# Expert outputs weighted at their PSUM copy and added to a sum in DRAM by accumulating indirect DMAs

## The reference, cut to what matters

```python
combine = route(h, w_router, router_bias)   # 512 x 16: two experts per token, weights sum to 1
ffn = 0
for e in range(16):                         # D_EXPERT = 256
    a = silu(h @ w_gate[e]) * (h @ w_up[e])
    ffn = ffn + combine[:, e:e + 1] * (a @ w_down[e])
ple = sigmoid(h @ w_ple_gate) * (p @ w_ple_proj)
x = layer_norm(alpha * h + ffn + ple, g, b)
```

## Time and profile before

| | us |
|---|---|
| runs (three) | 538.92, 539.41, 539.88 |
| span of the profiled execution, the only time known of it | 537.8 |
| PE busy | 479.0 (89%) |
| DVE busy | 312.9 (58%) |
| ACT busy | 170.4 (32%) |
| POOL busy | 145.7 (27%) |
| DMA | 98.95 MB, mean 184 GB/s |

### The profile page before, as it was taken

The page is one execution under the profiler, slowest core; times in us unless marked ns, Lnnn a source line. Parts: engine busy times, 40 slices in busy tenths (PEclk is TensorE's granted clock), DMA queues, the critical chain, the costliest instruction groups (busy, mean ns, idle before and its releaser), DMA issues.

```text
span 537.8 us, 4916 instructions
## 1 busy us (share of the span) xinstructions
PE 479.0 (89%) x1742; PEld 271.6 (50%) x1742; DVE 312.9 (58%) x516; ACT 170.4 (32%) x259; POOL 145.7 (27%) x138
## 2 busy tenths in 40 slices
PE   6999959999998999999999999899999999998100
PEld 2444436456853454444345444666766766675000
DVE  0289995934596226675072223477667757756197
ACT  0310002033569500003000003655555465452061
POOL 5018300360197550002000640023223223201032
PEclk9999979999999989999998999999999999999755
DMA  8991014212788591012700036699999999600353
GB/s 281 377 287 25 0 39 55 48 24 90 285 293 334 202 402 41 39 40 68 283 1 1 0 71 257 214 340 357 332 357 370 334 346 375 247 18 14 137 220 157
DMA packets 37303, 98.95 MB, mean 184 GB/s; under 512 B 16960, under 2 KB 22672, under 8 KB 30864
## 3 DMA queue, kind: packets, MB, share of 16 engines
q1 hardware_dynamic: 28272, 88.50, 45.3%
q0 software_dynamic: 5088, 8.49, 4.6%
q10 hardware_dynamic: 3920, 1.66, 1.4%
HBM read 91.18 MB, written 14.17 MB: 196 GB/s over the span
## 4 chain that ended last, share of the span: by engine, by line
PE 69%; DVE 19%; DMA 5%; ACT 3%; issue 3%; SPq 1%; DVEq 0%; POOLq 0%; ACTq 0%
PE bank L992 11%; PE bank L921 10%; PE bank L1069 8%; PE bank L1049 8%; PE bank L798 4%; PE bank L1055 3%; PE bank L1034 3%; PE bank L781 3%; PE bank L1057 3%; DMA region_b<-in_ssm_par 3%; PE bank L995 3%; PE bank L845 2%; PE bank L1052 2%; DVE region_f L1556 2%; PE bank L915 1%
## 5 line engine op out<-in xcount | busy, mean ns | idle before, releaser
L992 PE MATMUL bank<-region_c,region_g 128*128 128x512 f32 x128 | 58.2, 609 | 0.0
L921 PE MATMUL bank<-region_b,region_e 128*128 128x512 f32 x128 | 57.7, 609 | 0.0
L781 PE MATMUL bank<-region_e,region_a 128*128 128x512 f32 x128 | 55.4, 593 | 0.0
L992 PEld LDWEIGHTS bank<-region_c,region_g 128*128 128x128 f32 x128 | 24.6, 195 | 30.7 <-issue 30.7
L921 PEld LDWEIGHTS bank<-region_b,region_e 128*128 128x128 f32 x128 | 24.6, 195 | 29.6 <-issue 29.6
L781 PEld LDWEIGHTS bank<-region_e,region_a 128*128 128x128 f32 x128 | 24.2, 190 | 30.2 <-issue 29.9
L495 POOL DMA_INDIRECT region_e<-h_scratch,tok_t x16 | 27.2, 1703 | 18.1 <-PE bank L1034 9.4
L1049 PE MATMUL bank<-region_a,region_g 128*128 128x512 f32 x64 | 28.9, 595 | 2.0 <-ACT tokens_upper L708 1.3
L458 POOL TENSOR_SCALAR region_b<-region_b,vec 128x1024 f32<-128x1024 f32 x8 | 22.9, 2882 | 27.9 <-DMA region_b<-in_w_out 27.9
L500 POOL DMA_INDIRECT expert_scratch<-region_g,inv_t x8 | 7.9, 992 | 75.9 <-DVE region_g L1487 75.9
L1055 PE MATMUL bank<-gate_up_upper,tokens_lower 128*128 128x512 f32 x64 | 26.7, 417 | 1.4 <-DVE gate_up_lower L1504 1.4
(11 more groups left out here) (297 smaller groups left out, 942.7 us busy)
## 6 DMA issues: line engine op xcount, KB each, us to landing
region_a<-in_w_exp_gate SPq DMA_DIRECT2D x8, 1024.0 KB, 8.8
region_a<-in_w_exp_up SPq DMA_DIRECT2D x8, 1024.0 KB, 13.4
region_a<-in_w_exp_down SPq DMA_DIRECT2D x8, 1024.0 KB, 8.4
region_a<-in_w_in SPq DMA_DIRECT2D x3, 1536.0 KB, 16.7
region_b<-in_w_out SPq DMA_DIRECT2D x1, 4096.0 KB, 13.9
region_c<-in_w_ple_gate SPq DMA_DIRECT2D x1, 4096.0 KB, 14.9
region_b<-in_w_exp_gate SPq DMA_DIRECT2D x4, 1024.0 KB, 9.2
region_b<-in_w_exp_up SPq DMA_DIRECT2D x4, 1024.0 KB, 13.3
```

Source lines behind the costliest of these rows:

```text
L781: last = mm(bank[bank_i][:], w[:, k, m * P:(m + 1) * P], xT[:, k, :], start=(k == 0), stop=(k == KD - 1))
L921: last = mm(bank[WO_AT[half][group]][:], hdT[:, k, t * P:(t + 1) * P], w_o[:, k, half * 512:half * 512 + 512], start=(i == 0), stop=(i == ...
L992: last = mm(bank[PG_AT[k % 2]][:], hT[:, c, t * P:(t + 1) * P], w_pg[:, c, cols], start=(c == 0), stop=(c == KD - 1))
```

## The change

DRAM gets `sum_scratch` (`z_d`), 512 rows for tokens and 128 for pads, in the place of `expert_scratch`. A slot's record has two words, the token and its weight: the eight indirect DMAs write both, and an unused slot of partition p has the token 512 + p and the weight 0. SP stores alpha h + ple, tile by tile, to `z_d` before the experts' results come. DVE multiplies an expert's output by the slot's weight while it copies it from PSUM. POOL adds the rows to `z_d` by an indirect DMA with an addition; one add is issued after the one before it has landed. At the end SP loads four tiles of 512 KB, DVE takes mean and variance by `bn_stats` and `bn_aggr`, ACT takes the roots and normalises tiles 0 and 1, and POOL does the gain of tiles 0 and 1 and the bias of tile 0. The overflow rounds change in the same way.

```diff
-        inv_d = dram("slot_scratch", (SLOT_TILES * P, 1), I32)
-        ye_d = dram("expert_scratch", (2 * T, D))
+        inv_d = dram("slot_scratch", (SLOT_TILES * P, 2), I32)
+        z_d = dram("sum_scratch", (T + P, D))
...
+            def store_sum(t):
+
+                sp.wait_ge(S["ple_done"], 2 * t + 2)
+                sp.dma_start(z_d[t * P:(t + 1) * P, :], xh[:, t, :]).then_inc(S["z_out"], 16)
+
+            for t in range(NT - 1):
+                store_sum(t)
             sp.wait_ge(S["pe_pg"], 2 * NT)
             load_expert(3, 3)
+            store_sum(NT - 1)
...
             sp.wait_ge(S["moe_done"], 1)
-            yv = ye_d.rearrange("(t p k) d -> t k p d", p=P, k=2)
             for t in range(NT):
-                for k in range(2):
-                    sp.dma_start(RA[:, (2 * t + k) * D:(2 * t + k + 1) * D], yv[t, k]).then_inc(S[f"yk{k}_in{t}"], 16)
-            for t, signal, count in ((0, "o_pool", 1), (2, "o_dve", 1), (3, "o_dve", 2), (1, "o_dve", 3)):
+                sp.dma_start(xh[:, t, :], z_d[t * P:(t + 1) * P, :]).then_inc(S[f"z_in{t}"], 16)
+            for t, signal, count in ((2, "o_dve", 1), (3, "o_dve", 2), (0, "o_pool", 1), (1, "o_dve", 3)):
...
+            link(g.iota(rec_t[:, :, :, 0], pattern=[[P, NT], [0, 2]], base=0, channel_multiplier=1))
+            link(g.memset(inv_w, 0.0))
+            link(g.iota(inv_t[:, :, 0], pattern=[[0, SLOT_TILES]], base=T, channel_multiplier=1))
...
-            gp.dma_start(inv_d.rearrange("(p c) o -> p (c o)", p=P), pad_t[:]).then_inc(S["inv_set"], 16)
...
             gp.wait_ge(S["rot_ready"], 1)
+            gp.dma_start(inv_d.rearrange("(c p) o -> p c o", p=P), inv_t[:], allow_slow_non_contiguous=True).then_inc(S["inv_set"], 16)
...
             link(g.memset(RE[:, :], 0.0))
+            gp.dma_start(z_d[T:T + P, :], hg[:, 3, :]).then_inc(S["z_pad"], 16)
...
-                        in_=io_t[:, 2 * i + k:2 * i + k + 1], in_offset=None,
+                        in_=rec_t[:, i, k, :], in_offset=None,
...
-            gp.dma_start(inv_t[:], inv_d.rearrange("(c p) o -> p (c o)", p=P), allow_slow_non_contiguous=True).then_inc(S["inv_back"], 16)
+            gp.dma_start(inv_t[:], inv_d.rearrange("(c p) o -> p c o", p=P), allow_slow_non_contiguous=True).then_inc(S["inv_back"], 16)
...
-            def scatter(idx, src, signal):
-                gp.indirect_dma_start(out=ye_d, out_offset=bass.IndirectOffsetOnAxis(ap=idx, axis=0),
-                                      in_=src, in_offset=None,
-                                      bounds_check=2 * T - 1, oob_is_err=False).then_inc(S[signal], 16)
-
-            gp.wait_ge(S["tok_ready"], 1)
+            def add_rows(idx, src, signal):
+                gp.indirect_dma_start(out=z_d, out_offset=bass.IndirectOffsetOnAxis(ap=idx, axis=0),
+                                      in_=src, in_offset=None, compute_op=ALU.add).then_inc(S[signal], 16)
+
+            gp.wait_ge(S["inv_back"], 16)
+            gp.wait_ge(S["z_pad"], 16)
             for t in range(NT):
                 gp.wait_ge(S[f"h_out{t}"], 16)
             for e in range(4):
-                gather(hg[:, e, :], tok_t[:, e:e + 1], f"hg_in{e}")
+                gather(hg[:, e, :], inv_t[:, e, 0:1], f"hg_in{e}")
             for e in range(NE):
                 if e + 4 < NE:
                     gp.wait_ge(S["pe_hgT"], e + 1)
-                    gather(hg[:, e % 4, :], tok_t[:, e + 4:e + 5], f"hg_in{e % 4}")
+                    gather(hg[:, e % 4, :], inv_t[:, e + 4, 0:1], f"hg_in{e % 4}")
+                if e == 0:
+                    gp.wait_ge(S["z_out"], 16 * NT)
+                else:
+                    gp.wait_ge(S[f"ye_out{(e - 1) % 4}"], 16 * ((e - 1) // 4 + 1))
                 gp.wait_ge(S["ye_evac"], e + 1)
-                scatter(inv_t[:, e:e + 1], y_e[e % 4], f"ye_out{e % 4}")
+                add_rows(inv_t[:, e, 0:1], y_e[e % 4], f"ye_out{e % 4}")
...
+            for t in range(2):
+                gp.wait_ge(S["xhat_done"], t + 1)
+                g.tensor_tensor(xh[:, t, :], xh[:, t, :], lng, ALU.mult).then_inc(S["gain_done"], 1)
+            gp.wait_ge(S["gain_done"], 1)
             g.tensor_tensor(xh[:, 0, :], xh[:, 0, :], lnb, ALU.add).then_inc(S["o_pool"], 1)
-            gp.wait_ge(S["xhat_done"], 2)
-            g.tensor_tensor(xh[:, 1, :], xh[:, 1, :], lng, ALU.mult).then_inc(S["gain_done"], 1)
...
-            def deviation(t):
+            a.preload_act_table(ACT.Sqrt)
+            for t in range(NT):
                 ac.wait_ge(S["z2_ready"], t + 1)
-                a.activation(RA[:, (8 + t) * D:(9 + t) * D], xh[:, t, :], ACT.Square, bias=ln_mv[:, t, 0:1],
-                             accum_out=ln_mv[:, t, 1:2]).then_inc(S["var2_done"], 1)
-                ac.wait_ge(S["var2_done"], t + 1)
-                a.activation(ln_rs[:, t, 0:1], ln_mv[:, t, 1:2], ACT.Sqrt, bias=eps_t[:], scale=1.0 / D).then_inc(S["ln2_sqrt"], 1)
-
-            def x_hat(t):
-                ac.wait_ge(S["rs2_ready"], t + 1)
-                a.activation(xh[:, t, :], xh[:, t, :], ACT.Identity, bias=ln_mv[:, t, 0:1], scale=ln_rs[:, t, 1:2]).then_inc(S["xhat_done"], 1)
-
-            deviation(0)
-            deviation(1)
-            x_hat(0)
-            deviation(2)
-            x_hat(1)
-            deviation(3)
+                a.activation(ln_rs[:, t, 0:1], ln_mv[:, t, 1:2], ACT.Sqrt, bias=eps_t[:]).then_inc(S["ln2_sqrt"], 1)
+                if t < 2:
+                    ac.wait_ge(S["rs2_ready"], t + 1)
+                    a.activation(xh[:, t, :], xh[:, t, :], ACT.Identity, bias=ln_mv[:, t, 0:1], scale=ln_rs[:, t, 1:2]).then_inc(S["xhat_done"], 1)
...
-                link(tt(wgt[:, k, :], wgt[:, k, :], wsum, ALU.mult))
+                link(tt(rec_w[:, :, k, 1], wgt[:, k, :], wsum, ALU.mult))
...
-            dv.wait_ge(S["inv_back"], 16)
-            ts(tok_t[:], inv_t[:], 1, None, ALU.arith_shift_right).then_inc(S["tok_ready"], 1)
...
-                v.tensor_copy(y_e[b][:, 0:512], bank[B_DN[0]][:])
-                v.tensor_copy(y_e[b][:, 512:1024], bank[B_DN[1]][:]).then_inc(S["ye_evac"], 1)
+                w = inv_w[:, e, 1:2] if isinstance(e, int) else inv_w[:, bass.ds(e, 1), 1]
+                ts(y_e[b][:, 0:512], bank[B_DN[0]][:], w, None, ALU.mult)
+                ts(y_e[b][:, 512:1024], bank[B_DN[1]][:], w, None, ALU.mult).then_inc(S["ye_evac"], 1)
...
+            dv.wait_ge(S["inv_back"], 16)
...
-            def combine(t):
-
-                for k in range(2):
-                    dv.wait_ge(S[f"yk{k}_in{t}"], 16)
-                    yk = RA[:, (2 * t + k) * D:(2 * t + k + 1) * D]
-                    link(stt(xh[:, t, :], yk, wgt[:, k, t:t + 1], xh[:, t, :], ALU.mult, ALU.add,
-                             accum_out=ln_st[:, t, 0:1] if k == 1 else None))
-                ts(ln_mv[:, t, 0:1], ln_st[:, t, 0:1], -1.0 / D, None, ALU.mult).then_inc(S["z2_ready"], 1)
+            def statistics(t):
+
+                dv.wait_ge(S[f"z_in{t}"], 16)
+                for half_ in range(2):
+                    link(v.bn_stats(ln_st[:, t, 6 * half_:6 * half_ + 6], xh[:, t, half_ * 512:half_ * 512 + 512]))
+                v.bn_aggr(ln_mv[:, t, :], ln_st[:, t, :]).then_inc(S["z2_ready"], 1)
 
             def scale_rows(t):
 
                 dv.wait_ge(S["ln2_sqrt"], t + 1)
                 link(v.reciprocal(ln_rs[:, t, 1:2], ln_rs[:, t, 0:1]))
-                tt(ln_mv[:, t, 0:1], ln_mv[:, t, 0:1], ln_rs[:, t, 1:2], ALU.mult).then_inc(S["rs2_ready"], 1)
-
-            combine(0)
-            combine(1)
+                stt(ln_mv[:, t, 0:1], ln_mv[:, t, 0:1], -1.0, ln_rs[:, t, 1:2], ALU.mult, ALU.mult).then_inc(S["rs2_ready"], 1)
...
             scale_rows(0)
-            combine(2)
+            statistics(2)
             scale_rows(1)
-            combine(3)
+            statistics(3)
...
-                link(stt(xg, xh[:, t, :], ln_mv[:, t, 0:1], lng, ALU.add, ALU.mult))
+                link(stt(xg, xh[:, t, :], ln_mv[:, t, 0:1], lng, ALU.subtract, ALU.mult))
...
-            dv.wait_ge(S["gain_done"], 1)
+            dv.wait_ge(S["gain_done"], 2)
```

More of the change, by code:

```diff
@@ L47 @@
 SLOT_TILES = NE + OVER
-PAD = 4096
 ROUND = 1.5 * 2.0 ** 23
@@ L221, in trunk @@
         eps_t = sb("eps_t", [P, 1])
-        io_t = sb("io_t", [P, 2 * NT], I32)
-        pad_t = sb("pad_t", [P, SLOT_TILES], I32)
+        rec_t = sb("rec_t", [P, NT, 2, 2], I32)
         slot_i = sb("slot_i", [P, 2 * NT], I32)
-        inv_t = sb("inv_t", [P, SLOT_TILES], I32)
-        tok_t = sb("tok_t", [P, SLOT_TILES], I32)
+        inv_t = sb("inv_t", [P, SLOT_TILES, 2], I32)
         cur_t = sb("cur_t", [P, 2], I32)
+        rec_w = rec_t[:].bitcast(F32)
+        inv_w = inv_t[:].bitcast(F32)
+        cur_w = cur_t[:].bitcast(F32)
         over_i = sb("over_i", [1, 8], I32)
@@ L242, in trunk @@
             "pe_glu s_read s_max p_exp p_norm pt_evac pv_evac sq_done sq_added pe_sq rms_sqrt wo_scaled x_scaled wo_read pe_wo "
```

(25 more changed lines are left out.)

6 lines of the change are left out of this document (3 added, 3 removed).

## The result

The changed kernel takes 540.89 us (median of 20 runs, 539.79 to 543.72) against 539.67 for the kernel before on the same chips: ratio 1.003, 95% interval 1.0018 to 1.0042. By the ratio that is 1.6 us slower (1.0 to 2.3; the medians differ by 1.2), where 2.3 us faster was forecast. The time lies in the wide range of 533.5 to 548, which covered all rivals, but outside the forecast's own 535 to 540.5, and the sign was wrong.

A forecast was written before the change was run, and what follows sets the result against it. TensorE was taken to bound the expert loop, with everything after the last scatter exposed. Loop +2.1, adds in the loop 0, tail -4.4 (last adds' +2.1 included): -2.3 us, 539.41 to 537.1; own range 535 to 540.5, wide 533.5 to 548.

The forecast's parts named there:

- loop: operand and address: VectorE's weighted evacuations in the expert loop: +0.9 us for the per-partition operand, +1.2 for the register address, together +2.1.
- adds at the end: After the last experts: the last add waits for the one before and lands later, +2.1 us.
- tail from the first reload: Final norm after the expert loop: four reloads instead of eight and fewer operations shorten the stretch from 32.0 to 25.5 us.
- an unloaded add over 8 us: Sign named for a wrong prediction: an accumulating scatter without weight streaming takes over 8 us to land.
- `bn_stats` stretched: Sign named for a wrong prediction, in the tail: VectorE's statistics operation runs longer beside GpSimd.
- the slack: Expert loop, between VectorE's gate_up_lower and the matmul needing it: 0.07 us, said to take back some 0.8 of 1.7 us.
- Keeping pace: Adds in the expert loop: landing in 11.1 us against an expert's 10.39, lag covered by early gathers, cost 0.
- +1.9 per add: Each accumulating scatter: doubled rows and a second read per row add 1.9 us, taken nearest to measured DMA engine time.
- (B): Rival, expert loop: the chain of adds replaces TensorE as the bound, 546 us with adds of 12.5 us; chance 0.33.
- (C): Rival: adds cost only doubled rows and dearer evacuations vanish in TensorE's waits, -5.8 us, 533.6; chance 0.13.
- (D): Rival: evacuation at its upper bound of 4.9 us in the loop cancels the tail's gain, 539.9, no change; chance 0.12.
- The rest at nothing: Slot table's writes and read-back, pad rows' store, base sum's stores, gather index: no cost while covered, else 1 to 2 us each.

The follow-up runs named there:

- e1: The changed kernel with the expert loop's two evacuations as plain copies again, the weight left out (output unweighted): ratio 0.9971 to the kernel before.
- e2: The changed kernel with the weight operand always read from column 0, a fixed address (wrong weights): ratio 1.0004 to the kernel before.
- e8: The changed kernel with the weight applied to the activation product and plain copies at the evacuation, everything computed: ratio 0.9973 to the kernel before.
- e3: The changed kernel with plain scatters of all 128 rows, one after the other, nothing added (output wrong): ratio 0.9961 to the kernel before.
- e4: The changed kernel with accumulating scatters that drop their pad rows by a bounds check, everything computed: ratio 1.0048 to the kernel before.
- f2: The kernel before with one edit, its 128 x 1 row scale taking a per-partition operand instead of a second SBUF tensor: ratio 1.0001.
- e5: The changed kernel with SP's four output stores in the order the tiles are done, 0, 2, 3, 1: ratio 1.0009 to the kernel before.
- e6: e5's kernel with the row scale of tiles 0 and 1 taking a per-partition operand instead of a second SBUF tensor: ratio 0.9971 to the kernel before.

## Why the prediction was wrong, by its steps

| Step | predicted, us | measured, us |
|---|---|---|
| loop: operand and address | +2.1 | +2.9 |
| adds at the end | +2.1 | +3.3 |
| tail from the first reload | -6.5 | -4.4 |
| sum | -2.3 | +1.8 |

(The -4.4 of the prediction held the adds' +2.1; that the tail alone measured -4.4 is chance.) Of the 4.1 us by which the sum was off, the tail has 2.1, the adds 1.2 and the loop 0.8; any one of them alone would have left a gain. Neither sign that the prediction named for being wrong (an unloaded add over 8 us, `bn_stats` stretched) came up: they were set too wide to catch this.

- **Loop.** Mechanism right (e1, e2, e8), size off. Operand 14 x 0.12 = 1.7 was right: 1.84. The address, put at 1.2, measured 0.8. The failed term is the slack: I read 0.07 us between VectorE's end at 406.25 and the matmul at 406.32 and let it swallow 0.8 us (14 x 0.07 would even be 1.0). It swallowed nothing: experts that are written out went from 10.32 to 10.47, the whole 0.12 and a little. The matmul's weight load had been waiting 0.42 us for VectorE when it started at 406.30, as its row above shows, so those hundredths were the hand-over itself. The remaining +0.3 us lies between the last transposes and the last evacuation.
- **Keeping pace.** Right. An add under load lands after 10.4 us, 10.6 with the wait, against 11.1 forecast; the gathers' cover absorbs the lag, and though the DMA engines are 1.00 busy the loop isn't bound by them.
- **Adds at the end.** The term "+1.9 per add" was mis-sized and wrongly derived: it took time of the DMA engines for time to landing. An unloaded accumulate lands 2.9 us later than a plain scatter of the same rows (e3), as late with half of them (e4), and rows alone add 0.1 us. The last add is issued 1.2 us later behind its evacuation instead of 0.2, and takes 2.05 longer to land instead of 1.9. The prediction's two bounds for it (+0.6 and +10) held.
- **Tail.** The exclusion of VectorE and GpSimd was foreseen for the large operations and not for the small one, though it took 2.16 us in the tail of before to which the earlier trace rows belong (its row, 519.26, stands above f2's). It costs 1.5 us (e5 against e6). The last store cost another 1.3: I carried over the 3.24 us between the last operation and the end without looking at the new order of the stores. e5 and e6 show both: 27.6 to 26.3 to 24.8. That is 0.7 below the 25.5 forecast; the last reload landed 1.2 us sooner behind the first issue than I had put it (7.6 instead of 8.8), though no run shows that this is the 0.7.
- **Rivals.** (B) did not happen: an expert's counted traffic went to 3.7 MB (350 GB/s over 10.57 us), not to 4.3. The trace exceeds the rate that (B) quotes only in slices of a microsecond; its means are 339 GB/s before and 350 after. Nor did (C) happen. (D), the gain of the tail lost in the loop, was closest in kind, but its condition, a dear register address, wasn't met (0.8 against the 3.2 of its bound); the rest came from the adds' latency and the smaller gain of the tail. It had a chance of 0.12 and was held to no change.
- **The rest at nothing** fits, but no run tests it: the expert loop starts 1.2 us sooner than before, the clock's 1.7 us one way and 0.5 of scatter the other. The slot table's read-back, put at a microsecond or two, took 5.0 us to land in the profile of before.

## What to carry to other kernels

An engine that ends just as its dependent starts is on the critical path: look for a wait of the dependent's weight load before calling the gap slack, price every addition to the engine in full, and look for a place in its round where the same work lies beside a long operation of the bound engine. A serial chain of accumulating DMAs with nothing beside it pays its latency once per link; count links, not bytes, and don't take the DMA engines' busy time for the time to landing. In a tail with no cover, read the smallest operations and the order of the stores with the same care as the large ones, and before moving work to GpSimd ask whether VectorE will read two SBUF tensors meanwhile.

## What the runs showed of the hardware, unexpected

- An accumulating indirect DMA to DRAM: 6.1 to 6.4 us from issue to landing with 128 rows of 4 KB (changed kernel, after 475 us) and 6.1 with about 64 (e4); a plain one 3.3 (e3) and 3.2 (before). GpSimd is busy 1.55 us with its issue instead of 0.95. The 16 DMA engines' busy time does go with the rows: 12.0% of the span on queue 0, 7.5% with half the rows, 6.9% with all rows and no addition.
- An operand address that depends on a loop register costs VectorE 0.10 to 0.12 us ahead of the operation: 10.57 against 10.47 us per expert when it stands on the path, and nothing in the loop's time when it doesn't (e8).
- A store of 512 KB issued right behind another landed in 4.1 us (changed kernel), and in e6, 0.4 us behind another, in 3.6; apart from each other each took 2.6 to 2.8.
- VectorE's 128 x 1 operation on two SBUF tensors took 2.09 us beside GpSimd's multiplication, with a per-partition operand in place of the second 0.21, and `bn_stats` wasn't held up.
